# Band attention by pairs of heads: score products over 64 array rows, keys stored once, four buffers for the turned probabilities

## What is computed

```python
def windowed_gqa_sink(h, w_qkv, w_o, sink, rel_bias):   # 16 query heads, 4 key heads, 64 wide
    ...
    k_band = jnp.concatenate([kp[:, :-2], kp[:, 1:-1], kp[:, 2:]], axis=2)
    v_band = jnp.concatenate([vp[:, :-2], vp[:, 1:-1], vp[:, 2:]], axis=2)
    scores = jnp.einsum('bnqhgd,bnkhd->bnhgqk', q, k_band).astype(jnp.float32) * (dh ** -0.5)
    ...
    logits = jnp.where(mask[None, :, None, None], scores + bias[None, None], jnp.float32(-1e30))
    ...
    p = jax.nn.softmax(jnp.concatenate([logits, sink_l], axis=-1), axis=-1)[..., :-1]
    out = jnp.einsum('bnhgqk,bnkhd->bnqhgd', p.astype(v_band.dtype), v_band)
    return out.reshape(B, S, ATT_Q_HEADS * dh) @ w_o
```

## Time and profile before

| | us |
|---|---|
| median of 3 runs | 3573.45 (3573.07 to 3573.51) |
| the profiled execution's own time | 3573.72 |
| its span | 3572.0 |
| PE busy | 3073.5 (86%) |
| DVE busy | 1613.8 (45%) |
| ACT busy | 1364.6 (38%) |
| POOL busy | 778.5 (22%) |

### The profile page before, as it was taken

The page is one execution under the profiler, slowest core; times in us unless marked ns, Lnnn a source line. Parts: engine busy times, 40 slices in busy tenths (PEclk is TensorE's granted clock), DMA queues, the critical chain, the costliest instruction groups (busy, mean ns, idle before and its releaser), DMA issues. The chain is left out here.

```text
span 3572.0 us, 41010 instructions
## 1 busy us (share of the span) xinstructions
PE 3073.5 (86%) x14663; PEld 2446.1 (68%) x14663; DVE 1613.8 (45%) x2481; ACT 1364.6 (38%) x2009; POOL 778.5 (22%) x389
## 2 busy tenths in 40 slices
PE   6999977699877999674998989899998969799994
PEld 4777756488756877453666668777776856688883
DVE  6443467433453334523322231133334123799997
ACT  3333331444224432222333332122212113689995
POOL 1111001244323443110000002212211211244341
PEclk8999988799988999887999999999999989899997
DMA  5000042233522326210000012210101232578774
GB/s 208 31 18 6 1 171 112 65 100 94 177 94 82 100 78 210 107 41 22 15 15 7 7 42 70 78 37 34 47 23 59 75 114 108 193 257 274 269 257 147
DMA packets 83334, 343.20 MB, mean 96 GB/s; under 512 B 21045, under 2 KB 27477, under 8 KB 72225
## 3 DMA queue, kind: packets, MB, share of 16 engines
q1 hardware_dynamic: 63000, 316.64, 25.4%
q0 software_dynamic: 17856, 16.85, 2.2%
q10 hardware_dynamic: 2376, 8.46, 0.7%
HBM read 375.84 MB, written 45.69 MB: 118 GB/s over the span
## 5 line engine op out<-in xcount | busy, mean ns | idle before, releaser
L2461 DVE TENSOR_TENSOR ex_g_lo<-ex_g_raw,ex_g_hi 128x1024 fp32r<-128x1024 f32 x188 | 221.1, 1218 | 0.7 <-ACT ex_g_hi L2401 0.5
L2401 ACT CAST ex_g_hi<-ex_g_raw 128x1024 fp32r<-128x1024 f32 x188 | 191.8, 1052 | 14.7 <-PEq L1918 13.4
L618 DVE TENSOR_TENSOR ff_gated<-psum,ff_silu 128x512 f32<-128x512 f32 x44 | 30.4, 692 | 313.6 <-PE psum L490 313.6
L490 PE MATMUL psum<-ff_h_hi,ff0i_w_hi 128*128 128x512 f32 x352 | 137.9, 392 | 23.3 <-POOLq L443 23.3
L490 PE MATMUL psum<-ff_h_hi,ff1i_w_hi 128*128 128x512 f32 x352 | 138.0, 392 | 23.0 <-POOLq L443 23.0
L446 POOL TENSOR_TENSOR ff0i_w_lo<-ff0i_w_raw,ff0i_w_hi 128x1024 fp32r<-128x1024 f32 x43 | 106.4, 2473 | 211.9 <-ACT ff0i_w_hi L414 211.9
L2344 PE MATMUL psum<-ex_g_hi,ex_x_hi 128*128 128x512 f32 x376 | 150.8, 401 | 0.0
L977 ACT ACTIVATE ba_probs<-ba_logits,ba_stats 128x385 f32<-128x385 f32 (+1 forms) x128 | 75.6, 590 | 193.5 <-DVE ba_stats L1022 193.1
L446 POOL TENSOR_TENSOR ff1i_w_lo<-ff1i_w_raw,ff1i_w_hi 128x1024 fp32r<-128x1024 f32 x43 | 106.3, 2473 | 188.3 <-ACT ff1i_w_hi L414 188.3
L2345 PE MATMUL psum<-ex_g_lo,ex_x_hi 128*128 128x512 f32 x376 | 146.9, 391 | 0.0
L2346 PE MATMUL psum<-ex_g_hi,ex_x_lo 128*128 128x512 f32 x376 | 146.8, 391 | 0.0
(11 more groups left out here) (543 smaller groups left out, 8504.9 us busy)
## 6 DMA issues: line engine op xcount, KB each, us to landing
ex_g_raw<-in_w_experts_gu_dram SPq DMA_DIRECT2D x32, 2048.0 KB, 7.8
ex_d_raw<-in_w_experts_d_dram SPq DMA_DIRECT2D x32, 1024.0 KB, 9.9
ff0i_w_raw<-in_ffn_in_dram SPq DMA_DIRECT2D x44, 512.0 KB, 3.6
ff1i_w_raw<-in_ffn_in_dram SPq DMA_DIRECT2D x44, 512.0 KB, 3.6
wom_w<-in_mod_w_dram SPq DMA_DIRECT2D x8, 2048.0 KB, 8.0
ff0o_w_raw<-in_ffn_out_dram SPq DMA_DIRECT2D x16, 704.0 KB, 4.4
ff1o_w_raw<-in_ffn_out_dram SPq DMA_DIRECT2D x16, 704.0 KB, 4.2
ga_w_raw<-in_w_merge_a_dram SPq DMA_DIRECT2D x16, 512.0 KB, 3.6
```

Source lines behind the costliest of these rows:

```text
L490: mm = nc.tensor.matmul(chip.psum[:, 2 * u + h, :], w[:, v % 2, k * P:(k + 1) * P], (a[u] if isinstance(a, tuple) else a)[:, c * n_kc + k, ...
L2401: nc.scalar.copy(cols(g_hi, n), cols(raw.g_raw[i % 3], n)).then_inc(q["g_hi_made"], 1)
L2461: nc.vector.tensor_tensor(cols(g_lo, n), cols(raw.g_raw[i % 3], n), cols(g_hi, n).bitcast(F32), ALU.subtract).then_inc(q["g_lo_made"], 1)
```

## The change

The loops of all engines go by pairs of units (p = 0 to 15): two heads of one block, which share a q tile. In step p PE has the scores of pair p, the transposes of pair p - 1 and the value products of pair p - 2; ACT has both exponentials of pair p, then both copies of pair p - 1; DVE has the logits of pair p, then the scaling of pair p - 2. Keys are stored once as projected, `kd` (128 x 1024, the key head twice); a score product takes 64 partitions of q and of `kd`, 0 to 63 for the first head of a pair and 64 to 127 for the second. The zeros and their wait are gone. `ba_pt` has four places. The projections come in the order q tile 0, keys, q tile 1 (the host orders the weights so), in banks 4, 0 and 2, and the first scores wait for the first two copies only. The next group's first projection stands behind the last value products.

```diff
-    pt = chip.place("ba_pt", [P, 2, BAND], F32, FREE_AT + 12 * KIB + 512)
+    pt = [chip.place(f"ba_pt{u}", [P, 2, BAND], F32, at) for u, at in enumerate((FREE_AT + 12 * KIB + 512, B_AT + 12 * KIB))]
...
-    BANKS = (4, 2, 0)
+    BANKS = (4, 0, 2)
...
-                for u in range(NU + 10):
-                    if more and u in (6, 10, 14):
-                        split_hi(g + 1, (6, 10, 14).index(u))
-                    if u < NU:
...
+                for p in range(NP + 3):
+                    if more and p in (3, 5, 7):
+                        split_hi(g + 1, (3, 5, 7).index(p))
+                    for u in (2 * p, 2 * p + 1):
+                        if u < NU:
...
+                    for t in (2 * p - 2, 2 * p - 1):
+                        if 0 <= t < NU:
+                            w = band(t // HPG)[1] * P
+                            act.wait_ge(turned, NU * g + t + 1)
+                            nc.scalar.copy(pt[t // 2 % 2][:, t % 2, 0:w], chip.psum[:, 6 + t % 2, 0:w]).then_inc(pt_made, 1)
...
-            nc.vector.memset(kz[DH:P, 0, :], 0.0).then_inc(zeroed, 1)
-            nc.vector.memset(kz[0:DH, 1, :], 0.0).then_inc(zeroed, 1)
...
-                    if m < 2:
-                        nc.vector.tensor_copy(q[:, m, :], src).then_inc(qk_ready, 1)
-                    else:
-                        nc.vector.tensor_copy(kz[0:DH, 0, :], src[0:DH, :]).then_inc(qk_ready, 1)
-                        nc.vector.tensor_copy(kz[DH:P, 1, :], src[DH:P, :]).then_inc(qk_ready, 1)
+                    nc.vector.tensor_copy((q[:, 0, :], kd[:], q[:, 1, :])[m], src).then_inc(qk_ready, 1)
...
+                pe.wait_ge(scaled, NU * g + 2)
+                project_tile(g, 1)
                 pe.wait_ge(y_written, NB * g + 2)
-                project_tile(g, 1)
-                pe.wait_ge(scaled, NU * g + 2)
                 project_tile(g, 2)
...
+                for p in range(NP + 3):
+                    if p < NP:
+                        n, m = divmod(p, 2)
                         b0, nk, _ = band(n)
...
+                        if p < 2:
+                            pe.wait_ge(qk_ready, 3 * g + 2 + m)
+                        pe.wait_ge(logits, NU * g + 2 * p + 2)
+                        for i in range(2):
+                            rows = slice(i * DH, (i + 1) * DH)
+                            nc.tensor.matmul(chip.psum[:, 4 + i, 0:nk * P], q[rows, m, n * P:(n + 1) * P],
+                                             kd[rows, b0 * P:(b0 + nk) * P], start=True, stop=True).then_inc(scored, 1)
+                    for t in (2 * p - 2, 2 * p - 1):
...
+                    for w in (2 * p - 4, 2 * p - 3):
...
+                    if more and p == NP + 1:
+                        pe.wait_ge(logits, NU * g + NU + 2)
+                        project_tile(g + 1, 0)
+                    n = p // 2 - 2
+                    if n >= 0 and p % 2 == 0:
                         pe.wait_ge(scaled, NU * g + HPG * n + HPG + 2)
                         pe.wait_ge(y_written, NB * g + n + 1)
...
-            pe.wait_ge(zeroed, 2)
             project_tile(0, 0)
```

More of the change, by code:

```diff
@@ L969, in body @@
             def body(g, more):
-                for u in range(NU + 10):
-                    if more and u in (6, 10, 14):
-                        split_hi(g + 1, (6, 10, 14).index(u))
-                    if u < NU:
[L974 to L986, removed]
+                for p in range(NP + 3):
[3 more added lines that the diff above has]
+                        if u < NU:
+                            n, i = divmod(u, HPG)
+                            w = 1 + band(n)[1] * P
+                            act.wait_ge(negmax, NU * g + u + 1)
+                            nc.scalar.activation(pr[:, i, 0:w], lg[:, i, 0:w], ACT.Exp, bias=stats[:, NM, u % 8:u % 8 + 1],
+                                                 accum_out=stats[:, RS, u % 8:u % 8 + 1]).then_inc(probs, 1)
+                    for t in (2 * p - 2, 2 * p - 1):
[5 more added lines that the diff above has]
+                    if n >= 0 and p % 2 == 0:
                         act.wait_ge(o_turned, NB * g + n + 3)
@@ L1002, in body @@
                     src = chip.psum[:, BANKS[m]:BANKS[m] + 2, :].rearrange("p h t -> p (h t)")
-                    if m < 2:
-                        nc.vector.tensor_copy(q[:, m, :], src).then_inc(qk_ready, 1)
-                    else:
-                        nc.vector.tensor_copy(kz[0:DH, 0, :], src[0:DH, :]).then_inc(qk_ready, 1)
-                        nc.vector.tensor_copy(kz[DH:P, 1, :], src[DH:P, :]).then_inc(qk_ready, 1)
+                    nc.vector.tensor_copy((q[:, 0, :], kd[:], q[:, 1, :])[m], src).then_inc(qk_ready, 1)
                 dve.wait_ge(staged, 3 * g + 3)
-                for u in range(NU + 4):
-                    if u < NU:
+                for p in range(NP + 2):
+                    for u in (2 * p, 2 * p + 1):
+                        if u >= NU:
+                            continue
                         n, i = divmod(u, HPG)
@@ L1048, in body @@
             def body(g, more):
+                pe.wait_ge(scaled, NU * g + 2)
+                project_tile(g, 1)
                 pe.wait_ge(y_written, NB * g + 2)
-                project_tile(g, 1)
-                pe.wait_ge(scaled, NU * g + 2)
                 project_tile(g, 2)
[L1053 to L1058, removed]
-                        b0, nk, _ = band(n)
-                        if u == 0:
-                            pe.wait_ge(qk_ready, 4 * g + 4)
-                        pe.wait_ge(logits, NU * g + u + 1)
-                        nc.tensor.matmul(chip.psum[:, 4 + u % 2, 0:nk * P], q[:, i // 2, n * P:(n + 1) * P],
-                                         kz[:, i % 2, b0 * P:(b0 + nk) * P], start=True, stop=True).then_inc(scored, 1)
-                    t = u - 2
-                    if 0 <= t < NU:
+                for p in range(NP + 3):
+                    if p < NP:
+                        n, m = divmod(p, 2)
+                        b0, nk, _ = band(n)
+                        if p < 2:
[6 more added lines that the diff above has]
+                    for t in (2 * p - 2, 2 * p - 1):
+                        if not 0 <= t < NU:
+                            continue
                         i, nk = t % HPG, band(t // HPG)[1]
@@ L1073, in body @@
                         mm.then_inc(turned, 1)
-                    w = u - 3
-                    if 0 <= w < NU:
+                    for w in (2 * p - 4, 2 * p - 3):
+                        if not 0 <= w < NU:
+                            continue
                         b0, nk, _ = band(w // HPG)
@@ L1079, in body @@
                         for c in range(nk):
[L1080 removed]
+                            mm = nc.tensor.matmul(chip.psum[:, w % 2, 0:DH], pt[w // 2 % 2][:, w % 2, c * P:(c + 1) * P],
                                                   vg[:, b0 + c, :], start=(c == 0), stop=(c == nk - 1))
                         mm.then_inc(pv_done, 1)
[L1083 to L1085 removed]
+                    if more and p == NP + 1:
+                        pe.wait_ge(logits, NU * g + NU + 2)
+                        project_tile(g + 1, 0)
+                    n = p // 2 - 2
+                    if n >= 0 and p % 2 == 0:
                         pe.wait_ge(scaled, NU * g + HPG * n + HPG + 2)
```

17 lines of the change are left out of this document (7 added, 10 removed).

## The result

The changed kernel takes 3525.34 us, median of 4 runs (3520.14 to 3526.37), against 3573.26 (3572.68 to 3573.51): a ratio of 0.9863, 95% interval 0.9846 to 0.988. The forecast was 3531.0. It is 48 us faster, 5.7 us more than forecast. The profiled execution is the fastest of the four, 3520.14 us. Its span is 53.6 us shorter than the one before: the first projection starts 3.9 us earlier, the band attention is 52.1 us shorter, and the stages behind it take 2.4 us longer.

The account below looks back on a forecast made before the run. Latency of the chain through ACT's copy, not PE's work, was taken to set the period. Savings of 31.8 us in three groups, 8.9 in the last and 2.3 at the start, 43.0 off 3573.7, gave 3531 us; range 3512 to 3557.

Parts of the forecast that it names:

- What bounds the kernel: Band attention before the change: latency, not PE's work, sets the period; 50.0 us of work in 60.1 a group.
- Start: Ahead of the first projection: without the zeros PE need not wait for DVE; gain 2.3 us, between 2 and 2.6.
- Copies: Ahead of a group's first scores: q tile 0 and keys copied under later projections, so the 2.8 us pause goes.
- Four places: Steady loop: value products use copies made a pair step earlier, so PE's work, 3.28 us a pair, becomes the bound.
- Scores over 64 rows: A pair's scores: second head's first matmul runs beside first head's second, saving 0.32 us a pair, 4.7 a group.
- rival of whole overlap: A pair's scores: both heads run wholly together, a pair takes 3.0 us, the kernel 3514 us; chance 10%.
- Switches: Steady loop: PE changes between 128 and 64 rows twice a pair at 0.10 us each, costing 3.2 us a group.
- Filling and emptying: Group's ends: 2.8 us of stalls in the first steps, about 1.0 us waiting for copies at the last transposes.
- slower rival: Steady loop: each of three row changes a pair drains the array for 0.27 us, no overlap; 3589 us, chance 6%.

Follow-up runs that it names:

- units_late_pv: Kernel before with the value product one unit later (scaling and turned results too) and three places for the turned probabilities; 3551.4 us.
- changed_again: The changed kernel run once more without an edit, beside other kernels on one chip; 3525.7 us.
- two_places: Changed kernel with two places for the turned probabilities in place of four; 3526.3 us.
- same_rows: Changed kernel with both score products of a pair on rows 0 to 63, so neither head can overlap the other; 3689.1 us.
- full_rows: Changed kernel with both score products of a pair over all 128 rows, so no overlap and no change of rows; 3529.9 us.
- both: Changed kernel with ACT instead of DVE copying q tile 1 and the next group's first projection cut in two; 3524.9 us.
- full_both: The same two edits as both, but with score products over 128 rows against keys with zeros and two places for turned probabilities; 3524.9 us.

## Why the prediction was right, and where it wasn't

The time fell in the range, and the side and the size are right; the sum was 43 us and 48 came. By the chain of kernels the medians fall by 22 (value product later), 18 (order of projections), 3 (pairs) and 4 to 5 us (64 rows); the last two are hardly more than what separates kernels that didn't run beside each other. That 43 comes so near 48 is in part luck: several terms were off in both directions. Step by step:

- *What bounds the kernel.* Right: latency set the period. units_late_pv alone gives 22 us; my terms for it were the 10 us of stalls a group less 3.8 of filling and emptying, 25 in four groups. The 31 us of the earlier trace rows is not a time of PE: it adds the idle time of the weight loads (22.1) to that of PE itself (8.9) ahead of the same products. The sum didn't use it.
- *Start.* The first projection starts at 87.01, 3.9 us earlier; 2.3 were forecast. The term was right. PE stood idle for 3.27 us ahead of it, also in units_late_pv, and for 1.00 in the changed kernel and in changed_again: 2.3 less. The other 1.6 us arose ahead of that idle time and differ between traces: changed_again starts at 88.02, and units_late_pv, which waits for the zeros, at 88.97.

```profile
87.01 0.70 PE L1041 MATMUL psum<-h_hi,ba_w_hi 128*128 128x512 f32 x2 [1.00 <-PEq L723]
```

- *Copies.* Mis-sized. I had 2.8 us a group, 11 in all; 18 came, 16.5 of them in the band attention. I left out the clock behind the pause (0.57 to 0.72 for 4 us, 0.4 to 0.9 us a group) and the projections' wait for ACT's copy (0.6 in three groups); the 1 to 2 us that are left weren't separated.
- *Four places.* That ACT's copies would stop binding was right, and two_places shows that the order alone does it.
- *Scores over 64 rows.* Wrong. I had B1 beside A2 because matmuls start in program order; the trace has B1 7 ns behind A1. The rival of whole overlap, which I gave 10%, was the right one, and its saving of 0.64 us a pair is there: 0.32 us of columns twice in place of four times, and 0.65 by same_rows' last group. The sentence of the Trainium skill (TensorE: Matmul & The Clock Gate, Part 3: Packing small matmuls) on starts some 4 ns apart agrees, with 6 to 7 ns here; the use I made of the program order doesn't.
- *Switches.* Mis-sized in the other direction: 0.34 us a round trip, not 0.20. The step that failed was to take the rows as the whole price. They show the gap ahead of the new kind, not the delay behind it, which comes out only with a second matmul. The Trainium skill (TensorEngine Tiling, Key Properties) states that changing the tiling mode drains TensorE. The trace agrees, with a gap of 0.09 to 0.10 us at each change, and 0.10 and 0.05 more behind it. The two errors go against each other, which is luck: -0.64 + 0.34 = -0.30 a pair, forecast -0.12.
- *Whole overlap* was priced at 3514 us with P = 3.0. The pair is 3.05, so that was right; the time was not reached in any of the eight runs. The clock, which no case had, takes 2.5 us in the first trace and 8.5 in the second, about 1 us in most groups and 5 in one; and the shorter pair counts in nine steps of a group (full_rows), not in 12.
- *Filling and emptying.* Right. From the first scores to the fourth step's 7.7 us were measured (119.86 to 127.59), and 7.0 in the group that kept its clock, 7.3 forecast; the last transposes wait 1.0 us.

Of the slower rival (three changes of rows at 0.27 and no overlap) nothing came true in the changed kernel. The danger lay elsewhere: in same_rows, where 64-row products do not overlap, three of four groups ran at half clock.

## What to carry to other kernels

Where the list of waits shows PE's weight loads waiting for a copy of a unit issued just before, move the consumer one unit later first; that was worth 22 us here and took one more buffer (none in the order by pairs, as two_places shows). Fill the short pauses ahead of a burst by ordering the projections so that the operand needed first is copied under another's matmuls. Half-height products in two row groups pay only as far as what the burst saves (0.64 us here) outweighs the 0.34 us of a round trip, and they should be timed in several runs, for the median hides what they do to the clock.

## What was not expected of the hardware

- A float32 product's two matmuls over rows 0 to 63 and those of the next over rows 64 to 127 interleave: starts 142.80, 142.80, 143.22, 143.22.
- PE can be busy without a gap at half its clock: 98.00 of 98.00 us at 0.50 with 64-row score products that don't overlap, and 20.00 of 20.00 us at 0.50 in one group of `both`, where they do. With 128 rows the same loop held 1.00 in the traces of full_rows and full_both. full_rows and same_rows differ in the score products' rows alone, and with the rows come the changes between 64 and 128, so the two weren't wholly separated; but the changed kernel has as many changes and held 1.00 in its steady loop. It isn't certain to happen either: the last group of same_rows held 1.00, and why like groups differ was not explained.
- A pause of 2.6 us ahead of 128-row scores was followed by 0.57 to 0.72 for 4 us; stalls spread over the filling, over 128 rows, by 1.00.
